# The gated sum of a decoder layer's routed experts: the next tile's products made ahead of this tile's mean, the decode tile second, slot one-hots divided 4 and 4

## The chip, the cores and the metric

One core of one Trainium2 chip runs the whole program. The core has a matrix engine (TensorE, PE in the profile), a vector engine (VectorE, DVE), an activation engine (ScalarE, ACT), a general engine (GpSimd, POOL), a sequencer for transfers (SyncE, SP) and 16 DMA engines. Each engine runs its own queue of instructions in order; between engines there are semaphores. The metric is the device time of one execution in microseconds; the median of several runs counts.

## The reference

One step of a one-layer decoder for 512 prompt tokens and 8 decode tokens that share the weights. All is float32. Cut to what matters here:

```python
x = layernorm(DN_ALPHA * x + g1 * mix, ln1_g, ln1_b)      # mix: two gated linear recurrences, merged
h = x * (1.0 + sc2) + sh2
# router: 8 of 64 experts per token, gates w (n, 8)
routed, _ = lax.scan(expert, 0, (w_exp_gate, w_exp_up, w_exp_down, gates.T))
shared = (silu(t @ w_sh_gate) * (t @ w_sh_up)) @ w_sh_down
x = layernorm(DN_ALPHA * x + g2 * (routed + shared), ln2_g, ln2_b)
```

So at the end each token takes the sum of its eight experts' outputs, each times its gate, adds the shared expert's, multiplies by `g2`, adds its residual, and is normalized over the 1024 channels.

## The kernel before, in words

The program is written for each engine by hand: a block of code per engine, whose order is the order of that engine's queue. Tokens are kept as five tiles: tiles 0 to 3 of 128 prompt tokens each, tile 4 the 8 decode tokens. The residual `X` lies channel-major (128 partitions by 8 groups of channels by 520 tokens).

**Slots of the routed loop.** The router's choices are turned into a table that says which token's row each slot of the expert loop takes. For each of the five tiles DVE computes the slot numbers (L1983 to L1993); then for each of the 8 choices k a one-hot matrix over slots is made. `PK = 5` says that POOL makes those of k = 0 to 4 (L1446) and DVE those of k = 5 to 7 (L2000). DVE also makes one wide comparison per tile (L2002, `Boh`). PE multiplies the pairs (L1078): per tile it waits for all of DVE's and then for POOL's one after another. DVE copies the table out of PSUM (L2006) and finishes it; POOL's first gathers of token rows and the first steps of the loop need it. `Aoh` and `Boh` have two buffers, so from the third tile on DVE and POOL wait for PE's products of the tile two before.

**The routed loop** runs expert by expert on all engines and stores each token's eight rows to DRAM (`yrows`). The change does not touch it.

**The final stage** starts with PE's products of the shared expert (L1174), which ACT copies to `sums[t]` (L1385). SP loads the decode tokens' rows (L807) and then `picks[t]`, 4 MB per tile, into three buffers (L812); the fourth waits until DVE has taken its half of tile 0 and PE its own. The sum over the eight choices is divided, `NPE = 4`:

- PE's half (L1195), here "gated products": 32 products of `picks` with a diagonal matrix that POOL made of the gates (L1485), into PSUM banks 0/1 or 2/3 by turns. A float32 product shows as two instructions, so the profile has 64. ACT multiplies by `g2` ("scaling", L1391, 8 operations) and POOL adds to `X` ("POOL's addition", L1491).
- DVE's half (L2074, 4 operations over 1024 channels) goes into `sums[t]`. PE transposes it (L1203, 8 operations, banks 4 and 5), and DVE adds it to `X`, times `g2` ("residual", L2082).
- The decode tile: PE multiplies the 64 rows with gates and adds the shared part (L1183, L1184, bank 6); DVE adds it in two small operations (L2064, L2066).
- The normalization of a tile: PE sums over the channels ("mean", `mean_pe`, L490, bank 6), DVE subtracts ("centre", L712), ACT squares (L569), PE sums again ("variance", `variance_pe`, L490, bank 7), ACT takes the root ("deviation", L573), DVE takes the reciprocal (L717) and multiplies (L720, both "normalize"), ACT applies weight and bias ("affine", L580), SP stores the tile (L819). Of the last tile, which carries the 8 decode tokens too, DVE does half of the affine (L2091).

PE's queue before: decode products; then for each tile t gated products t, variance t-1, transposes t, mean t; at the end variance 3. The other engines have their queues in the same sense: DVE's is decode additions, then half t, normalize t-1, residual t, centre t; ACT's is scaling t, deviation t-1, affine t-1, square t.

Of the kernel before, what the change touches and what calls it, by code (L numbers as in the profile page):

```python
# [26 lines left out]
P = 128  # L27
D = 1024
KC = D // P
SEQ = 512  # L30
DEC = 8
NT = SEQ + DEC
# [96 lines left out]
def decoder_step(nc, xT, small, wgk2, const, route, wq, wexp, st_in, yT, st_prompt, st_out):  # L129
    with ExitStack() as ctx:  # L130
# [31 lines left out]
        def view(buf, first, n, pattern=None, **kw):  # L162
            v = buf[:, first:first + n]
            return v.rearrange(pattern, **kw) if pattern else v
# [240 lines left out]
            eng.wait_ge(s_hd[0], 48)  # L405
            eng.wait_ge(s_hd[1], 32)

        PK = 5

        def visits(i, big, small, k):  # L410

# [82 lines left out]
        def mean_pe(pe, t):  # L494
            pe.wait_ge(s_f3, t + 2)
            sum_pe(pe, t, X[:, :, TAIL[t]], 6)

        def variance_pe(pe, t):
            pe.wait_ge(s_lna, t + 5)
            sum_pe(pe, t, lsq2[:, t % 2, :, 0:wide_of(t)], 7)  # L500
# [66 lines left out]
        def square_act(act, t):  # L567
            act.wait_ge(s_ln, 3 * t + 1)
            act.activation(lsq2[:, t % 2, :, 0:wide_of(t)], X[:, :, TAIL[t]], ACT.Square).then_inc(s_lna, 1)  # L569

        def deviation_act(act, t):
            act.wait_ge(s_lnp, 2 * t + 6)
            act.activation(lnr2[:, t % 2, 0, 0:wide_of(t)], ps[:, 7, t % 2 * 256:t % 2 * 256 + wide_of(t)], ACT.Sqrt,  # L573
                           bias=C("eps")).then_inc(s_lng, 1)

        def affine_act(act, t):
            g, b = S("ln2_g"), S("ln2_b")
            act.wait_ge(s_ln, 3 * t + 3)
            for c in range(KC if t < 3 else KC // 2):
                act.activation(X[:, c, TAIL[t]], X[:, c, TAIL[t]], ACT.Identity, scale=g[:, c:c + 1],  # L580
                               bias=b[:, c:c + 1]).then_inc(s_laf, 1)
# [127 lines left out]
        def centre_dve(dve, t):  # L709
            x = X[:, :, TAIL[t]]  # L710
            dve.wait_ge(s_lnp, 2 * t + 5)
            dve.tensor_tensor(x, x, wide(ps[:, 6, t % 2 * 256:t % 2 * 256 + wide_of(t)]), ALU.subtract).then_inc(s_ln, 1)  # L712

        def normalize_dve(dve, t):
            x, dev, inv = X[:, :, TAIL[t]], lnr2[:, t % 2, 0, 0:wide_of(t)], lnr2[:, t % 2, 1, 0:wide_of(t)]
            dve.wait_ge(s_lng, 4 + t)
            dve.reciprocal(inv, dev).then_inc(s_ln, 1)  # L717
            dve.wait_ge(s_ln, 3 * t + 2)
            dve.wait_ge(s_lna, t + 5)
            dve.tensor_tensor(x, x, wide(inv), ALU.mult).then_inc(s_ln, 1)  # L720
# [104 lines left out]
        def _(pe):  # L825
# [349 lines left out]
                                       shWD[:, f, hf * 512:(hf + 1) * 512], start=(f == 0), stop=(f == 1))  # L1175
                    mm.then_inc(t_y, 1)

            pe.wait_ge(s_f1[4], 16)
            pe.wait_ge(s_dg, 1)
            pe.wait_ge(t_yc, 2)  # L1180
            for m in range(KC):
                part, o = slice(m * P, (m + 1) * P), ps[:, 6, m * DEC:(m + 1) * DEC]
                pe.matmul(o, pdec[0:DEC * TOPK, part], dsel[0:DEC * TOPK, :], start=True, stop=False)  # L1183
                mm = pe.matmul(o, sums[4][0:DEC, part], ident[0:DEC, 0:DEC], start=False, stop=True)  # L1184
            mm.then_inc(s_f2, 1)
            for t in range(4):
                pe.wait_ge(s_f1[t], 16)
                pe.wait_ge(s_dg, t + 2)
                if t < 2:
                    pe.wait_ge(t_yc, 2 * TT)  # L1190
                else:
                    pe.wait_ge(s_ea, t - 1)
                for m in range(KC):
                    for k in range(NPE):
                        mm = pe.matmul(ps[:, 2 * (t % 2) + m // 4, m % 4 * P:(m % 4 + 1) * P], picks[t % 3][:, k, m * P:(m + 1) * P],  # L1195
                                       diag[:, t, k, :], start=(k == 0), stop=(k == NPE - 1))
                mm.then_inc(s_pa, 1)
                if t:
                    variance_pe(pe, t - 1)
                pe.wait_ge(s_cmb, (TOPK - NPE) * (t + 1))  # L1200
                pe.wait_ge(s_f3, t + 1)
                for m in range(KC):
                    mm = pe.transpose(ps[:, 4 + m // 4, m % 4 * P:(m % 4 + 1) * P], sums[t][:, m * P:(m + 1) * P], ident)  # L1203
                mm.then_inc(s_f2, 1)
                mean_pe(pe, t)
            variance_pe(pe, 3)


        @block.scalar
        def _(act):  # L1210
# [170 lines left out]
            for j, t in enumerate((4, 0, 1, 2, 3)):  # L1381
                rows = min(P, NT - t * P)
                for hf in range(2):
                    act.wait_ge(t_y, 2 * j + hf + 1)
                    act.activation(sums[t][0:rows, hf * 512:(hf + 1) * 512], ps[0:rows, 2 * (j % 2) + hf, :], ACT.Copy)\  # L1385
                       .then_inc(t_yc, 1)
            for t in range(4):
                act.wait_ge(s_pa, t + 1)
                since(act, s_xa, t - 1)
                for m in range(KC):  # L1390
                    ins = act.activation(gated[:, t % 2, m, :], ps[:, 2 * (t % 2) + m // 4, m % 4 * P:(m % 4 + 1) * P], ACT.Copy,  # L1391
                                         scale=md[:, G2 + m, 0:1])
                ins.then_inc(s_ea, 1)
                if t:
                    deviation_act(act, t - 1)
                    affine_act(act, t - 1)
                square_act(act, t)
            deviation_act(act, 3)
            affine_act(act, 3)

# [96 lines left out]
        def _(dve):  # L1497
# [560 lines left out]
                        gate(dve, "dve", s_y, visits(i, 2, 1, k) + (7 + hf))  # L2058
                        dve.tensor_copy(yb[:, k % 2, hf * 512:(hf + 1) * 512], ps[:, 3 if k % 2 else 4 + hf, :]).then_inc(s_yc, 1)  # L2059

            dve.wait_ge(s_laf, KC)
            dve.wait_ge(s_f2, 1)
            dec = view(tiny, 64, KC * DEC, "p (c b) -> p c b", c=KC)
            dve.tensor_tensor(dec, ps[:, 6, 0:KC * DEC].rearrange("p (c b) -> p c b", c=KC), md[:, G2:G2 + KC, 1:NCOND], ALU.mult).then_inc(s_fy, 1)  # L2064
            dve.wait_ge(s_fy, 1)
            dve.tensor_tensor(X[:, :, SEQ:NT], X[:, :, SEQ:NT], dec, ALU.add).then_inc(s_f3, 1)  # L2066
            for t in range(4):
                dve.wait_ge(s_f1[t], 16)
                dve.wait_ge(t_yc, 2 * t + 4)
                for k in range(NPE, TOPK):  # L2070
                    n = (TOPK - NPE) * t + k - NPE
                    if k > NPE:
                        dve.wait_ge(s_cmb, n)
                    dve.scalar_tensor_tensor(out=sums[t], in0=picks[t % 3][:, k, :], scalar=gk[:, t, k:k + 1],  # L2074
                                             in1=sums[t], op0=ALU.mult, op1=ALU.add).then_inc(s_cmb, 1)
                if t:
                    normalize_dve(dve, t - 1)
                dve.wait_ge(s_f2, t + 2)
                dve.wait_ge(s_xa, t + 1)
                for m in range(KC):  # L2080
                    x = X[:, m, t * P:(t + 1) * P]
                    ins = dve.scalar_tensor_tensor(out=x, in0=ps[:, 4 + m // 4, m % 4 * P:(m % 4 + 1) * P], scalar=md[:, G2 + m, 0:1],  # L2082
                                                   in1=x, op0=ALU.mult, op1=ALU.add)
                ins.then_inc(s_f3, 1)
                centre_dve(dve, t)
            normalize_dve(dve, 3)
            dve.wait_ge(s_ln, 12)
            g, b = S("ln2_g"), S("ln2_b")
# [65 lines left out]
```

## Time and profile before

| | us |
|---|---|
| median of 3 runs | 1845.16 (1844.14 to 1849.97) |
| profiled execution, its own time | 1849.65 |
| its span | 1847.8 |
| PE busy in the span | 1705.9 (92%) |
| DVE busy | 579.9 (31%) |
| ACT busy | 458.7 (25%) |
| POOL busy | 302.6 (16%) |
| mean granted clock of TensorE | 0.962 |

The span goes from the first to the last instruction of one profiled execution; its own time is what the run took as a whole. The last 100 us of the span hold the final stage, the stretch from 1017 to 1052 us the slots. The granted clock is a share of 2.4 GHz: 1.00 is 2.4 and 0.50 is 1.2 GHz.

### The profile page before, as it was taken

The page shows a single profiled execution, that of the slowest core. Times are in us where ns is not written, and L with a number is a line of the kernel's source. Part 1 is how long each engine was busy: PE and PEld are TensorE (multiplying, and loading weights), DVE is VectorE, ACT ScalarE, POOL GpSimd, SP SyncE. Part 2 cuts the span into 40 slices and gives each one's busy share as a digit, 9 for nine tenths or more (in the row PEclk, how much of TensorE's full clock was granted, in tenths as well). Part 3 has the DMA queues.
Part 4 walks back from the last instruction along what each step waited for, and adds up shares of the span by engine and source line. Part 5 has one row for each costly group of instructions (what it writes and reads, how often), then busy time and mean ns, then how long its engine had stood idle before and what let it go on. Part 6 is the DMA issues. An engine that isn't in the chain of part 4 may idle for free.

```text
span 1847.8 us, 26405 instructions
## 1 busy us (share of the span) xinstructions
PE 1705.9 (92%) x8996; PEld 1132.6 (61%) x8996; DVE 579.9 (31%) x1489; ACT 458.7 (25%) x1040; POOL 302.6 (16%) x493
## 2 busy tenths in 40 slices
PE   5999789999999899799999599999999999999975
PEld 2854468577858788588887445455444544444575
DVE  1213750586048734200136711111111111111144
ACT  1314651464145433200002111111111111111223
POOL 0000110022001100000000722222222222222311
PEclk8999989999999999899999699999999999999987
DMA  9113441211120099454011489999999999998441
GB/s 397 78 46 131 176 162 46 92 48 43 55 92 3 9 401 342 167 231 167 22 69 47 158 337 411 416 404 400 397 408 403 401 397 394 369 386 351 196 195 35
DMA packets 57197, 410.31 MB, mean 222 GB/s; under 512 B 12955, under 2 KB 18716, under 8 KB 29986
## 3 DMA queue, kind: packets, MB, share of 16 engines
q1 hardware_dynamic: 36210, 365.65, 49.9%
q0 software_dynamic: 19184, 42.58, 6.0%
q10 hardware_dynamic: 1728, 1.05, 0.2%
q8 instruction: 51, 0.84, 0.2%
q14 instruction: 24, 0.20, 0.0%
HBM read 391.79 MB, written 42.07 MB: 235 GB/s over the span
## 4 chain that ended last, share of the span: by engine, by line
PE 71%; DMA 11%; DVE 9%; ACT 5%; issue 2%; POOL 2%; SPq 0%; POOLq 0%; ACTq 0%; DVEq 0%
PE ps L957 12%; PE ps L1116 11%; PE ps L916 9%; DMA arena<-wexp 8%; PE ps L894 6%; PE ps L1121 5%; PE ps L1140 5%; PE ps L1147 3%; PE ps L997 3%; DMA arena<-wq 2%; PE ps L865 2%; PE ps L1195 2%; DVE arena L1606 2%; ACT arena L625 2%; PE ps L1102 2%
## 5 line engine op out<-in xcount | busy, mean ns | idle before, releaser
L1116 PE MATMUL ps<-arena 128*128 128x512 f32 x592 | 266.0, 603 | 10.5 <-DMA arena<-wexp 9.1
L1116 PEld LDWEIGHTS ps<-arena 128*128 128x128 f32 x592 | 111.2, 193 | 151.9 <-issue 151.9
L916 PE MATMUL ps<-Hb,arena 128*128 128x260 f32 x768 | 173.5, 390 | 0.0
L916 PEld LDWEIGHTS ps<-Hb,arena 128*128 128x128 f32 x768 | 148.8, 194 | 24.1 <-ACT arena L1251 0.5
L2050 DVE TENSOR_TENSOR arena<-ps,arena 128x256 f32<-128x256 f32 x73 | 26.2, 359 | 418.4 <-ACT arena L1365 418.4
L1469 POOL DMA_INDIRECT yrows<-arena x72 | 74.6, 1036 | 429.7 <-issue 429.7
L957 PE MATMUL ps<-Hb,arena 128*128 128x260 f32 x512 | 124.0, 397 | 14.6 <-DMA arena<-wq 14.1
L1121 PE MATMUL ps<-arena 128*64 128x256 f32 x1152 | 132.3, 382 | 1.5 <-issue 0.9
L1140 PE MATMUL ps<-arena 128*128 128x512 f32 x288 | 129.6, 592 | 0.0
L2059 DVE COPY arena<-ps 128x512 f32<-128x512 f32 x108 | 74.7, 692 | 152.1 <-PE ps L1140 105.8
L957 PEld LDWEIGHTS ps<-Hb,arena 128*128 128x128 f32 x512 | 100.8, 198 | 32.5 <-DMA arena<-wq 14.8
L1365 ACT ACTIVATE arena<-ps 128x256 f32<-128x256 f32 x73 | 24.2, 332 | 377.4 <-PE ps L1116 260.5
L865 PE MATMUL ps<-Hb,arena 128*128 128x260 f32 x512 | 117.5, 383 | 0.0
L894 PE MATMUL ps<-arena,Hb 128*128 128x512 f32 x256 | 112.0, 595 | 0.0
L1121 PEld LDWEIGHTS ps<-arena 128*64 128x64 f32 x1152 | 82.2, 137 | 41.6 <-issue 7.7
L865 PEld LDWEIGHTS ps<-Hb,arena 128*128 128x128 f32 x512 | 94.8, 190 | 13.1
L1606 DVE TENSOR_TENSOR arena<-arena 128x256 f32<-128x256 f32 x168 | 60.1, 428 | 102.7 <-ACT arena L627 102.7
L894 PEld LDWEIGHTS ps<-arena,Hb 128*128 128x128 f32 x256 | 48.0, 190 | 64.2 <-issue 60.8
L1140 PEld LDWEIGHTS ps<-arena 128*128 128x128 f32 x288 | 51.9, 190 | 51.6 <-issue 51.6
L1358 ACT ACTIVATE arena<-ps 128x512 f32<-128x512 f32 x111 | 62.4, 595 | 41.3 <-PE ps L1102 39.5
L1460 POOL DMA_INDIRECT Hb<-h2rows,arena x58 | 62.5, 1078 | 49.6 <-POOL arena L1458 47.9
L1742 DVE TENSOR_TENSOR arena<-arena,ps 128x260 f32<-128x260 f32 x32 | 13.6, 425 | 179.3 <-PE ps L957 179.2
(339 smaller groups left out, 2262.9 us busy)
## 6 DMA issues: line engine op xcount, KB each, us to landing
arena<-wexp SPq DMA_DIRECT2D x73, 2048.0 KB, 16.2
arena<-wq SPq DMA_DIRECT2D x44, 2048.0 KB, 8.5
arena<-wexp SPq DMA_DIRECT2D x72, 1024.0 KB, 19.4
arena<-yrows SPq DMA_DIRECT2D x4, 4096.0 KB, 18.8
arena<-st_in SPq DMA_DIRECT2D x8, 1024.0 KB, 10.1
Xb<-vs POOLq DMA_DIRECT2D x16, 512.0 KB, 9.8
st_out<-arena SPq DMA_DIRECT2D x8, 1024.0 KB, 9.4
Xb<-xT SPq DMA_DIRECT2D x2, 2080.0 KB, 17.6
```

What stands on the lines that cost most here:

```text
L865: mm = pe.matmul(ps[:, bank, 0:HALF], ring[:, q % 4, m % 4, c, :], H[:, c, lo:lo + HALF], start=(c == 0), stop=(c == KC - 1))
L894: mm = pe.matmul(ps[:, bank, :], H[:, c, b * P:(b + 1) * P], ring[:, q % 4, :, c, :], start=(c == 0), stop=(c == KC - 1))
L916: mm = pe.matmul(ps[:, bank, 0:HALF], ring[:, q % 4, a, c, :], H[:, c, halves[b][0]:halves[b][1]], start=(c == 0), stop=(c == KC - 1))
L957: mm = pe.matmul(ps[:, 5 + k % 3, 0:HALF], ring[:, (Q_P + n) % 4, u, c, :], (H, oa, H, ob)[u][:, c, lo:hi], start=(c == 0), stop=(c == KC ...
L1116: mm = pe.matmul(ps[:, 0, :], xe[:, 0, c, :], GU[k % 4][:, c, :], start=(c == 0), stop=(c == KC - 1))
L1121: mm = pe.matmul(ps[h * SS:(h + 1) * SS, 1, 0:FE], x, GUs[k % 4][:, c, h, :, :], start=(c == 0), stop=(c == KC - 1), tile_position=(0, h * ...
L1140: mm = pe.matmul(ps[:, 4 + hf, :], aT[:, 0, f, :], WD[k % 4][:, f, hf * 512:(hf + 1) * 512], start=(f == 0), stop=(f == 1))
L1358: act.activation(xe[:, k % 2, 4 * hf:4 * hf + 4, :].rearrange("p c n -> p (c n)"), ps[:, 6 + hf, :], ACT.Copy).then_inc(s_xc, 1)
L1460: pool.indirect_dma_start(out=xg[k % 4][:, 0:n], out_offset=None, in_=rows, in_offset=bass.IndirectOffsetOnAxis(ap=idg[:, k % 4:k % 4 + 1] ...
L1469: pool.indirect_dma_start(out=rows, out_offset=bass.IndirectOffsetOnAxis(ap=ida[:, k:k + 1], axis=0), in_=yb[:, k % 2, 0:n], in_offset=Non ...
L1606: dve.tensor_tensor(e, e, kq, ALU.mult)
L2059: dve.tensor_copy(yb[:, k % 2, hf * 512:(hf + 1) * 512], ps[:, 3 if k % 2 else 4 + hf, :]).then_inc(s_yc, 1)
```

## The change

PE's queue becomes: gated products 0, transposes 0, decode products; then for t = 0 to 2 gated products t+1, variance t-1 (from t = 1), mean t, transposes t+1; then variance 2, mean 3, variance 3. DVE's becomes: half 0, residual 0, decode additions; then for t = 0 to 2 normalize t-1 (from t = 1), half t+1, centre t, residual t+1; then normalize 2, centre 3, normalize 3. ACT's becomes: scaling 0; then for t = 0 to 2 scaling t+1, deviation t-1 and affine t-1 (from t = 1), square t; then deviation 2, square 3, affine 2, deviation 3, affine 3. POOL's and SP's queues in the final stage stay. `PK` becomes 4: POOL makes the one-hots of k = 0 to 3, DVE those of k = 4 to 7.

```diff
--- before.py
+++ after.py
@@ -405,7 +405,7 @@
             eng.wait_ge(s_hd[0], 48)
             eng.wait_ge(s_hd[1], 32)
 
-        PK = 5
+        PK = 4
 
         def visits(i, big, small, k):
 
@@ -1175,15 +1175,7 @@
                                        shWD[:, f, hf * 512:(hf + 1) * 512], start=(f == 0), stop=(f == 1))
                     mm.then_inc(t_y, 1)
 
-            pe.wait_ge(s_f1[4], 16)
-            pe.wait_ge(s_dg, 1)
-            pe.wait_ge(t_yc, 2)
-            for m in range(KC):
-                part, o = slice(m * P, (m + 1) * P), ps[:, 6, m * DEC:(m + 1) * DEC]
-                pe.matmul(o, pdec[0:DEC * TOPK, part], dsel[0:DEC * TOPK, :], start=True, stop=False)
-                mm = pe.matmul(o, sums[4][0:DEC, part], ident[0:DEC, 0:DEC], start=False, stop=True)
-            mm.then_inc(s_f2, 1)
-            for t in range(4):
+            def gated_turn(t):
                 pe.wait_ge(s_f1[t], 16)
                 pe.wait_ge(s_dg, t + 2)
                 if t < 2:
@@ -1195,14 +1187,31 @@
                         mm = pe.matmul(ps[:, 2 * (t % 2) + m // 4, m % 4 * P:(m % 4 + 1) * P], picks[t % 3][:, k, m * P:(m + 1) * P],
                                        diag[:, t, k, :], start=(k == 0), stop=(k == NPE - 1))
                 mm.then_inc(s_pa, 1)
+
+            def sums_turn(t):
+                pe.wait_ge(s_cmb, (TOPK - NPE) * (t + 1))
                 if t:
-                    variance_pe(pe, t - 1)
-                pe.wait_ge(s_cmb, (TOPK - NPE) * (t + 1))
-                pe.wait_ge(s_f3, t + 1)
+                    pe.wait_ge(s_f3, t + 1)
                 for m in range(KC):
                     mm = pe.transpose(ps[:, 4 + m // 4, m % 4 * P:(m % 4 + 1) * P], sums[t][:, m * P:(m + 1) * P], ident)
                 mm.then_inc(s_f2, 1)
+
+            gated_turn(0)
+            sums_turn(0)
+            pe.wait_ge(s_f1[4], 16)
+            for m in range(KC):
+                part, o = slice(m * P, (m + 1) * P), ps[:, 6, m * DEC:(m + 1) * DEC]
+                pe.matmul(o, pdec[0:DEC * TOPK, part], dsel[0:DEC * TOPK, :], start=True, stop=False)
+                mm = pe.matmul(o, sums[4][0:DEC, part], ident[0:DEC, 0:DEC], start=False, stop=True)
+            mm.then_inc(s_f2, 1)
+            for t in range(3):
+                gated_turn(t + 1)
+                if t:
+                    variance_pe(pe, t - 1)
                 mean_pe(pe, t)
+                sums_turn(t + 1)
+            variance_pe(pe, 2)
+            mean_pe(pe, 3)
             variance_pe(pe, 3)
 
 
@@ -1384,17 +1393,24 @@
                     act.wait_ge(t_y, 2 * j + hf + 1)
                     act.activation(sums[t][0:rows, hf * 512:(hf + 1) * 512], ps[0:rows, 2 * (j % 2) + hf, :], ACT.Copy)\
                        .then_inc(t_yc, 1)
-            for t in range(4):
+            def gated_scale(t):
                 act.wait_ge(s_pa, t + 1)
                 since(act, s_xa, t - 1)
                 for m in range(KC):
                     ins = act.activation(gated[:, t % 2, m, :], ps[:, 2 * (t % 2) + m // 4, m % 4 * P:(m % 4 + 1) * P], ACT.Copy,
                                          scale=md[:, G2 + m, 0:1])
                 ins.then_inc(s_ea, 1)
+
+            gated_scale(0)
+            for t in range(3):
+                gated_scale(t + 1)
                 if t:
                     deviation_act(act, t - 1)
                     affine_act(act, t - 1)
                 square_act(act, t)
+            deviation_act(act, 2)
+            square_act(act, 3)
+            affine_act(act, 2)
             deviation_act(act, 3)
             affine_act(act, 3)
 
@@ -2058,13 +2074,7 @@
                         gate(dve, "dve", s_y, visits(i, 2, 1, k) + (7 + hf))
                         dve.tensor_copy(yb[:, k % 2, hf * 512:(hf + 1) * 512], ps[:, 3 if k % 2 else 4 + hf, :]).then_inc(s_yc, 1)
 
-            dve.wait_ge(s_laf, KC)
-            dve.wait_ge(s_f2, 1)
-            dec = view(tiny, 64, KC * DEC, "p (c b) -> p c b", c=KC)
-            dve.tensor_tensor(dec, ps[:, 6, 0:KC * DEC].rearrange("p (c b) -> p c b", c=KC), md[:, G2:G2 + KC, 1:NCOND], ALU.mult).then_inc(s_fy, 1)
-            dve.wait_ge(s_fy, 1)
-            dve.tensor_tensor(X[:, :, SEQ:NT], X[:, :, SEQ:NT], dec, ALU.add).then_inc(s_f3, 1)
-            for t in range(4):
+            def picks_sum(t):
                 dve.wait_ge(s_f1[t], 16)
                 dve.wait_ge(t_yc, 2 * t + 4)
                 for k in range(NPE, TOPK):
@@ -2073,16 +2083,32 @@
                         dve.wait_ge(s_cmb, n)
                     dve.scalar_tensor_tensor(out=sums[t], in0=picks[t % 3][:, k, :], scalar=gk[:, t, k:k + 1],
                                              in1=sums[t], op0=ALU.mult, op1=ALU.add).then_inc(s_cmb, 1)
-                if t:
-                    normalize_dve(dve, t - 1)
-                dve.wait_ge(s_f2, t + 2)
+
+            def resid_sums(t):
+                dve.wait_ge(s_f2, t + 1 + (t > 0))
                 dve.wait_ge(s_xa, t + 1)
                 for m in range(KC):
                     x = X[:, m, t * P:(t + 1) * P]
                     ins = dve.scalar_tensor_tensor(out=x, in0=ps[:, 4 + m // 4, m % 4 * P:(m % 4 + 1) * P], scalar=md[:, G2 + m, 0:1],
                                                    in1=x, op0=ALU.mult, op1=ALU.add)
                 ins.then_inc(s_f3, 1)
+
+            dve.wait_ge(s_laf, KC)
+            picks_sum(0)
+            resid_sums(0)
+            dve.wait_ge(s_f2, 2)
+            dec = view(tiny, 64, KC * DEC, "p (c b) -> p c b", c=KC)
+            dve.tensor_tensor(dec, ps[:, 6, 0:KC * DEC].rearrange("p (c b) -> p c b", c=KC), md[:, G2:G2 + KC, 1:NCOND], ALU.mult).then_inc(s_fy, 1)
+            dve.wait_ge(s_fy, 1)
+            dve.tensor_tensor(X[:, :, SEQ:NT], X[:, :, SEQ:NT], dec, ALU.add).then_inc(s_f3, 1)
+            for t in range(3):
+                if t:
+                    normalize_dve(dve, t - 1)
+                picks_sum(t + 1)
                 centre_dve(dve, t)
+                resid_sums(t + 1)
+            normalize_dve(dve, 2)
+            centre_dve(dve, 3)
             normalize_dve(dve, 3)
             dve.wait_ge(s_ln, 12)
             g, b = S("ln2_g"), S("ln2_b")
```

## Rows read from the trace of the kernel before

**Rows 1.** Chain of waits from 1700 us: start, us, engine, tile, line, count

```profile
1748.03 0.32 PE ps L1183 x2
...
1753.80 9.69 PE ps L1195 x64
...
1763.52 2.19 ACT arena L1391 x8
...
1765.85 2.35 POOL Xb L1491
...
1768.29 2.17 DVE Xb L2082 x8
...
1770.51 3.78 PE ps L490 x16
...
1784.41 1.28 ACT L573
...
1804.60 0.27 ACT arena L573
...
1813.71 7.16 PE ps L1195 x64
```

**Rows 2.** PE's timeline: start, us, line, shapes, count, [idle before, releaser]

```profile
1763.32 1.04 PE L1203 MATMUL ps<-cst,Hb 128*128 128x128 f32 x8
...
1782.02 1.95 PE L490 MATMUL ps<-arena,cst 128*128 128x128 f32 x16
```

**Rows 3.** DVE's timeline, same columns

```profile
1754.32 5.24 DVE L2074 SCALAR_TENSOR_TENSOR Hb<-arena,OB,Hb 128x1024 f32<-128x1024 f32 x4
...
1774.33 1.22 DVE L712 TENSOR_TENSOR Xb<-Xb,ps 128x1024 f32<-128x1024 f32 x1 [3.87 <-PE ps L490]
...
1787.10 1.23 DVE L720 TENSOR_TENSOR Xb<-Xb,arena 128x1024 f32<-128x1024 f32 x1
...
1804.89 0.95 DVE L717 RECIPROCAL arena<-arena 128x128 f32<-128x128 f32 x1 [4.25 <-ACT arena L573]
1805.88 2.22 DVE L720 TENSOR_TENSOR Xb<-Xb,arena 128x1024 f32<-128x1024 f32 x1
```

**Rows 4.** ACT's timeline, same columns

```profile
1815.01 1.06 ACT L569 ACTIVATE arena<-Xb 128x1024 f32<-128x1024 f32 x1 [3.69 <-DVE Xb L712]
...
1842.02 1.67 ACT L580 ACTIVATE Xb<-Xb,sml 128x136 f32<-128x136 f32 x4 [2.40 <-DVE Xb L720]
```

**Rows 5.** Stretches: us, busy PE, PEld, DVE, ACT, POOL, granted clock, DMA share, GB/s

```profile
1748.00:1751.90 3.90, 3.90 (x27) 3.65 (x26) 0.00 (x0) 0.60 (x1) 0.00 (x0) 0.99 0.96 412
1751.90:1758.70 6.80, 6.80 (x31) 6.70 (x32) 4.64 (x6) 0.00 (x0) 0.00 (x0) 0.50 0.99 424
...
1769.00:1775.70 6.70, 5.20 (x24) 5.20 (x25) 2.83 (x8) 0.12 (x1) 0.00 (x0) 0.50 1.01 433
1813.40:1821.00 7.60, 7.60 (x70) 7.60 (x70) 6.27 (x5) 1.16 (x2) 0.00 (x0) 1.00 0.13 38
```

**Rows 6.** DMA issues at 1734.67 and 1735.30 (tiles 0, 1): KB, us to landing

```profile
arena<-yrows SPq DMA_DIRECT2D x1, 4096.0 KB, 14.0
...
arena<-yrows SPq DMA_DIRECT2D x1, 4096.0 KB, 23.0
```

**Rows 7.** One-hots: timelines of POOL, DVE, PE, and line L1446 (ns min/median/max)

```profile
1019.64 25.99 POOL L1446 TENSOR_SCALAR arena<-OB 128x128 f32<-128x128 f32 x25 [4.63 <-DVE OB L1993]
...
L1446 POOL TENSOR_SCALAR arena<-OB x25: 785/787/2127, 1019.6 to 1044.8; 128x128 f32<-128x128 f32 x25
...
1034.22 0.99 DVE L2000 TENSOR_SCALAR arena<-OB 128x128 f32<-128x128 f32 x3 [1.11 <-PE ps L1078]
...
1039.81 1.29 DVE L2002 TENSOR_TENSOR arena<-OB 128x1088 f32<-128x1088 f32 x1
1047.93 0.30 DVE L2006 COPY OB<-ps 128x136 f32<-128x136 f32 x1 [6.83 <-PE ps L1078]
...
1041.81 6.08 PE L1078 MATMUL ps<-arena 128*128 128x136 f32 x24 [1.12 <-POOL arena L1446]
```

## The prediction, as it was made

> **What bounds the kernel now.** The last 100 us are a chain over all four engines, and PE, the busiest engine of the kernel as a whole, waits in it. I read the chain of waits from 1748 us on first, then each engine's timeline there, the granted clock by stretches, the landings of the four loads, and last the stretch of the one-hots at 1019 to 1048 us.
>
> Chain, tile 0 [rows 1]: decode products from 1748.03 to 1753.80 (5.77 us), gated products 9.69, scaling on ACT 2.19, POOL's addition 2.35, DVE's residual 2.17, PE's mean products 3.78; only then tile 1's gated products. PE's own work between tile 0's gated products and that mean is 1.04 us of transposes [rows 2]: it stood idle from 1764.4 to 1770.5, and so for each tile, and its clock paid for it. In 1769.0 to 1775.7 the grant is 0.50, that is 1.2 GHz, behind such a pause; in 1813.4 to 1821.0 it is 1.00, 2.4 GHz, and 64 gated products take 7.16 us [rows 1, 5]. At 1.2 GHz sixteen mean products take 3.78 us, at 2.4 sixteen variance products 1.95 with their drain [rows 1, 2]; I use 1.75 in a filled queue, half of 3.5. The clock falls a first time at 1751.9 inside the decode products, which have 8 columns each, and so tile 0's gated products took 9.69 instead of 7.16 [rows 1, 5].
>
> The divided sum's other half, DVE's 5.24 us per tile, is always done before PE's transposes ask for it [rows 3]. The one-hots: POOL runs 25 of them without a gap for 25.99 us, DVE ends its last at 1041.1, and PE's last products at 1047.9 come behind POOL's [rows 7].
>
> **The change, part by part.** I follow the new order instruction by instruction, with the clock as these rows have it.
>
> Start. Tile 0's gated products need only tile 0's rows, landed at 1734.67+14.0=1748.67 [rows 6], ACT's copies of the shared product, which end right behind PE's, and POOL's diagonals, made long before. They start at 1748.75, directly behind wide products, so at 2.4 GHz: 7.16, to 1755.9. DVE starts its half at 1748.75 too and is done at 1754.0. Transposes 0.95, to 1756.9. Decode products: 0.315 us a pair at 2.4 GHz [rows 1], 16 pairs, 5.0, to 1761.9. Beside them run scaling (to 1758.1), POOL (to 1760.6) and DVE's residual (to 1762.8): the decode tile fills PE's pause instead of standing first. DVE's two decode additions (0.5) end at 1763.3.
>
> Tile 1's gated products start at 1761.9; their rows landed at 1735.30+23.0=1758.3 [rows 6], so no DMA wait. To 1769.1; mean of tile 0 (1.75) to 1770.8; transposes to 1771.8 (DVE's half: 1763.3 to 1768.6). Tile 2's gated products follow at once, to 1778.9, its rows should land 9.6 us behind tile 1's, at 1767.9 (an estimate from the two landings). Then variance 0 and mean 1, to 1782.4; DVE finished residual 1 at 1776.0, behind scaling and POOL.
>
> Here the new order stops giving. The first deviation comes after variance 0 and after scaling 2 (1781.1), with the table load of 1.28 [rows 1]: 1782.8. DVE has normalize 0 ahead of its half of the sum for tile 2: 0.96+1.23 [rows 3], to 1785.0, then 5.24, to 1790.3. PE's transposes of tile 2 wait for that, and behind them tile 3's products: a pause of 7.9 us. The clock will fall in it, as it did in the pause of 6.1. So transposes 1.9, to 1792.2, and gated products 3 partly at 1.2 GHz: 9.2, between 7.2 and 9.7 of [rows 1], to 1801.4. From tile 0's gated start to tile 3's it was 59.9 us, 20.0 a tile; now it is 43.4. Scaling 2.2, deviation 0.3 [rows 1], reciprocal, and a multiplication that takes 2.22 instead of 1.23 because POOL's addition lies on it [rows 3]: 1807.3. DVE's half for tile 3 to 1812.5; transposes, again after 7.6 us of pause, to 1814.5; residual 3 to 1816.7. Variance 2 (3.5, at 1.2 GHz) fills that, to 1818.4, and mean 3 needs 2.7, to 1821.2. Centre 1.22, square 1.06 [rows 3, 4], to 1823.5. Now ACT has affine 2 ahead of deviation 3: eight pieces at twice the 1.67 us of four [rows 4], about 3.2, to 1826.7; it covers variance 3 at either clock, which otherwise is 4.0. Deviation 0.36 and normalize 2.2: 1829.3. Before, that multiplication ended at 1842.0, and 5.8 us followed, which stay. The tail wins **12.7 us**.
>
> One-hots. POOL gives up 5 of 25, DVE takes 5 at about 0.29 (three cost 0.86 to 0.99) [rows 7]. POOL then needs per tile 4 times 0.787 plus the 1.34 by which DVE's wide comparison and product stretch one of its operations (2.127 against 0.787), some 4.7 with small change; DVE's 4.6 becomes 4.9. DVE's wait of 1.11 for PE [rows 7] goes, since PE is no longer held by POOL. So DVE's last comparison ends at 1041.1+5x0.29-1.11=1041.4, and PE needs for the last tile's 16 products two thirds of 6.08, 4.05 us: 1045.5 against 1047.9. The bounds: a loss of 0.3 (the 1.45 moved less 1.11), if what is late is DVE, and a gain of 3.5, if PE runs these at 2.4 GHz and only POOL's last operation, at about 1043.3, holds it. I take **2.4**, from PE's row. What follows it hangs on DVE's copy at 1047.93, gathers and expert loads alike, so the routed loop should start earlier by all of it; where the loop later waits for its loads, those were also asked for earlier.
>
> Of this the Trainium skill speaks in "GPSIMD Engine Reference", section Key points: GpSimd shares its SBUF interfaces with VectorE and contends with Vector instructions in a 2-port mode or with two SBUF inputs. The two-input side is what the 2127 ns row shows. If the moved one-hots contend as fully, the sum by the rule has no 2.4.
>
> Clock in front of tile 1. With transposes and decode products between tile 0's and tile 1's wide products, 6.0 us without a wide product, against 3.9 us from 1748.0 until the fall at 1751.9 before [rows 5], I expect it to fall there again. Tile 1's products then take 9.7, not 7.2: **2.5 back** (0 to 2.5).
>
> Sum: 1849.65 (profiled, span 1847.8 and 1.85 around it) - 12.7 - 2.4 + 2.5 = 1837.05; I say **1837.0**. The profiled execution is 4.5 above the median 1845.16 of the runs shown. I don't take that off: these runs spread over 5.8 us, which falls of the clock at shifting places of the tail would give (1.8 to 2.5 each), and the new order has fewer chances for luck. Against the median it is 8.2 us, 0.44%.
>
> **The rivals.**
> (a) The one-hots bring nothing. For: POOL's operations are stretched up to 2.7 times by DVE's. With 4x0.29 more stretch a tile, POOL needs 3.15+1.34+1.15=5.6, five tiles 28, as late as now. Against: the 25 took 25.99, 6.3 above 25x0.787, and one operation stretched by 1.34 in each of five tiles is all of that. Time 1839.4.
> (b) The tail only hides the decode tile: the ring of gated products, scaling, deviation, normalize, DVE's half, transposes is 7.2 to 9.7 + 2.2 + 0.3 + 2.2 to 3.2 + 5.2 + 1 to 1.9 = 18 to 22.5, hardly shorter than the 20.0 per tile of before. I have it twice; if it bound three times, another 6 go: 1843. For: DVE's order puts normalize ahead of the half. Against: in the first turns nothing there waits for a deviation.
> (c) Slower: PE's two pauses of almost 8 us, longer than the 6 of before, leave it at 1.2 GHz through what follows. Place: tile 1, tile 3, variance 1 and mean 2. Price: gated products at 14.3 each, 4.6 and 5.1 more, 3.5 for variance and mean, and with it one more pair for tile 2 (7.2): 20 us, 1857. It decides from 13.7 us of such loss (8.2 forecast + 5.5). Against: the two stretches at 0.50 in [rows 5] lasted 6.8 and 6.7 us, with PE at work again for 6.8 and 5.2 of them.
> (d) The change does not move the tail, because mean 0 still waits for residual 0 behind the decode additions: 0.5 us of DVE, no more; 1847.
>
> **How the numbers follow.** Forecast 0.58 (1833 to 1840), (a) 0.14, (b) 0.18, (c) 0.05, (d) 0.05. A difference under about 0.3%, 5.5 us, cannot be told from none here, so faster means below 1839.6: the forecast nearly whole, half of (a): 0.65. Within: the rest of (a), (b), part of (d): 0.27. Slower: (c) and a remainder: 0.08. Range for 8 in 10: 1831.5 (clock stays up before tile 1, one-hots at 3.5, half the median's lead) to 1844 (b).
>
> **What would show it.** Right: gated products 0 at about 1746 beginning at once behind the shared ones, lasting 7.2; decode products inside POOL's and DVE's time; three sets of gated products within 31 us; two PE pauses of 7 to 8 us ended by DVE's half of the sum; ACT's affine 2 ahead of the last deviation; DVE's table copy near 1045.5. Wrong: a pause ahead of tile 1's products, gated products of 14 us, or a copy still near 1048.

## The result and the profile after

The changed kernel takes 1832.09 us (median of 4 runs, 1830.96 to 1832.85), the kernel before beside it 1844.65. The ratio is 0.9924 with a 95% interval of 0.9907 to 0.9941, that is 14 us faster (11 to 17); the medians lie 12.6 apart. A second set of runs (below) gave 0.9934 (0.9919 to 0.9949). Forecast were 1837.0 and a gain of 8.2 us: the sign is right, the gain is half as large again, and the time lies at the lower end of the range, 1831.5 to 1844. Put on the median of 1845.16 that the forecast stood beside, the ratio gives 1831.1, just below it.

Two lines of the page of the changed kernel:

```profile
span 1828.9 us, 26402 instructions
...
PE 1690.9 (92%) x8996; PEld 1121.6 (61%) x8996; DVE 579.2 (32%) x1494; ACT 458.1 (25%) x1040; POOL 298.9 (16%) x488
```

Its profiled execution took 1830.96 us. Against the 1849.65 of before that is 18.7 less. Of the 18.9 by which the spans differ, 6.4 are ahead of the final stage (the last shared product ends at 1741.6, not 1748.0 [rows 1]) and 12.5 are in it (from there to the end of the span 87.3, not 99.8). Of the 6.4, 1.2 are there before the slots begin, 2.7 are the slots' (below), and 2.5 come in the routed loop, which is unchanged.

The chain of waits of the changed kernel, which answers to [rows 1] (start, us, engine, tile, line, count; L1187 are the gated products, L1196 the transposes, L490 mean and variance, L1400 scaling, L2084 DVE's half, L573 on ACT deviation, L712 centre, L720 normalize):

```profile
1742.38 7.38 PE ps L1187 x64
1749.76 0.87 PE ps L1196 x8
...
1755.66 8.93 PE ps L1187 x64
1764.60 1.79 PE ps L490 x16
1766.38 0.87 PE ps L1196 x8
1767.26 7.16 PE ps L1187 x64
...
1774.44 2.17 ACT arena L1400 x8
...
1776.63 1.28 ACT L573
...
1784.41 1.29 DVE Hb L2084
...
1785.75 1.97 PE ps L1196 x8
1787.72 8.15 PE ps L1187 x64
...
1804.12 1.30 DVE Hb L2084
...
1809.00 2.60 PE ps L490 x16
...
1811.63 0.38 ACT arena L573
...
1814.24 1.21 DVE Xb L712
...
1816.63 3.70 PE ps L490 x16
...
1820.36 0.38 ACT arena L573
...
1821.80 1.30 DVE Xb L720
```

Tile 0's gated products start behind the shared ones and take 7.38 us, not 9.69. Tiles 1 and 2 follow without one wait of PE's for another engine; tile 2's begin 24.9 us behind tile 0's. Then the chain leaves PE, through the first deviation, normalize and DVE's half, and does so again for tile 3. PE's timeline has both pauses in brackets:

```profile
1776.03 1.95 PE L490 MATMUL ps<-Xb,cst 128*128 128x128 f32 x16
1785.75 1.97 PE L1196 MATMUL ps<-cst,Hb 128*128 128x128 f32 x8 [7.77 <-DVE Hb L2084]
...
1806.78 1.97 PE L1196 MATMUL ps<-cst,Hb 128*128 128x128 f32 x8 [7.35 <-DVE Hb L2084]
```

They are 7.77 and 7.35 us; forecast were 7.9 and 7.6. The granted clock of four stretches (us; then busy time of PE, PEld, DVE, ACT, POOL; clock; DMA share; GB/s):

```profile
1742.40:1749.70 7.30, 7.30 (x65) 7.30 (x66) 3.78 (x3) 0.00 (x0) 0.00 (x0) 1.00 1.00 429
1755.60:1758.90 3.30, 3.30 (x16) 3.30 (x16) 3.23 (x9) 0.00 (x0) 0.00 (x0) 0.50 1.08 467
1759.00:1764.50 5.50, 5.50 (x51) 5.50 (x51) 3.20 (x3) 0.00 (x0) 0.00 (x0) 1.00 0.96 408
1782.90:1789.50 6.60, 3.75 (x18) 3.75 (x19) 5.59 (x11) 1.92 (x4) 0.00 (x0) 0.50 0.27 79
```

At 2.4 GHz through tile 0's products, at 1.2 behind the decode products (8.93 for tile 1, forecast 9.7), and at 1.2 again from inside the first pause on, until 1789.5. These rows answer to [rows 5].

The one-hots (POOL's timeline; then the line in ns, min/median/max; then DVE's timeline and PE's), against [rows 7]:

```profile
1018.42 23.25 POOL L1462 TENSOR_SCALAR arena<-OB 128x128 f32<-128x128 f32 x20 [4.61 <-DVE OB L2009]
...
L1462 POOL TENSOR_SCALAR arena<-OB x20: 784/830/2495, 1018.4 to 1040.9; 128x128 f32<-128x128 f32 x20
...
1037.09 1.26 DVE L2016 TENSOR_SCALAR arena<-OB 128x128 f32<-128x128 f32 x4
1038.18 1.28 DVE L2018 TENSOR_TENSOR arena<-OB 128x1088 f32<-128x1088 f32 x1
1044.01 0.30 DVE L2022 COPY OB<-ps 128x136 f32<-128x136 f32 x1 [4.54 <-PE ps L1078]
...
1041.73 2.24 PE L1078 MATMUL ps<-arena 8*128 8x136 f32 x10 [0.28 <-POOL arena L1462]
```

The first slot number is there at 1018.04 (1019.25 before, both by DVE's timeline). From there to the table copy L2022 it is 1044.01-1018.04=26.0 us, before 1047.93-1019.25=28.7: 2.7 less, with 2.4 forecast.

### The profile page after: what moved, and what is told of

It reads as the page before. It is cut to its first block, busy times and chain, and to the rows that moved or that the text cites. A ratio compares the mean times of both kernels' runs of the same rounds, so it can differ in the third digit from the quotient of the medians.

```text
span 1828.9 us, 26402 instructions
## 1 busy us (share of the span) xinstructions
PE 1690.9 (92%) x8996; PEld 1121.6 (61%) x8996; DVE 579.2 (32%) x1494; ACT 458.1 (25%) x1040; POOL 298.9 (16%) x488
## 4 chain that ended last, share of the span: by engine, by line
PE 69%; DMA 12%; DVE 9%; ACT 5%; issue 2%; POOL 2%; SPq 0%; POOLq 0%; ACTq 0%; DVEq 0%
PE ps L957 12%; PE ps L1116 11%; PE ps L916 9%; DMA arena<-wexp 9%; PE ps L894 6%; PE ps L1121 5%; PE ps L1140 5%; PE ps L1147 3%; PE ps L997 3%; PE ps L865 2%; DVE arena L1622 2%; ACT arena L625 2%; PE ps L1187 2%; ACT arena L627 2%; PE ps L1102 2%
## 6 DMA issues: line engine op xcount, KB each, us to landing
Xb<-xT SPq DMA_DIRECT2D x2, 2080.0 KB, 17.6
```

## The experiments

**The two parts alone.** One is a single line:

```diff
-        PK = 5
+        PK = 4
```

> The kernel before with PK = 4 alone. Theory A (the one-hots are worth the 2.4 us forecast and the loop behind them keeps it): the table copy some 2.7 us earlier against the first slot number of tile 0, and a median 2 to 4 us below the kernel before, about 1841.5. Theory B (the one-hots bring nothing, the loop waits for its loads all the same): within 1 us of the kernel before.

Measured: 0.9985 of before (0.9975 to 0.9995), 2.8 us less (0.9 to 4.6); medians 1842.46 and 1845.51. POOL's and DVE's timelines in it (L1993 the first slot number, L2006 the table copy):

```profile
1019.78 23.17 POOL L1446 TENSOR_SCALAR arena<-OB 128x128 f32<-128x128 f32 x20 [4.62 <-DVE OB L1993]
...
1019.40 0.17 DVE L1993 SCALAR_TENSOR_TENSOR OB<-OB 128x8 f32<-128x8 f32 x1
...
1045.10 0.30 DVE L2006 COPY OB<-ps 128x136 f32<-128x136 f32 x1 [4.36 <-PE ps L1078]
```

25.7 us between the two, against 28.7. Theory A holds: the loop keeps what the slots give, and rival (a) is out, by its interval only just.

> The changed kernel with PK = 5, so only the order of the final stage is new. Theory A (the sum of the prediction holds, 12.7 less 0 to 2.5 for the clock in front of tile 1): 9 to 12 us below the median of the kernel before, about 1834.5; from PE's last shared product to the end of the span about 87.5 us. Theory B (the reordered tail is worth only the hidden decode tile): 6 us below, about 1839.

Measured: 0.9952 (0.9940 to 0.9964), 8.9 us less (6.6 to 11.1), median 1836.80. From the last shared product to the end 90.9 us in its trace. That lies between the two: A had 9 to 12 us and 87.5 for the stage, B had 6 us, and the interval leaves B out only just. The parts, 2.8 and 8.9, add up to 11.7.

**The changed kernel again.**

> The changed kernel once more on this chip, for its place beside the others. Theory A (sum of the prediction taken from the usual time of the kernel before instead of its first profiled execution: 1845.5 - 12.7 = 1832.8, 1 to 2 more with the clock): 1831 to 1835. Theory B (its first four executions were lucky as the first of before was unlucky): 1835 to 1838.

Measured: 1833.93 (1830.63 to 1835.06), 0.9934, or 12.2 us less (9.4 to 15). Its final stage took 89.3 us, with tile 1's products at 9.98. Theory A, though its sum leaves the one-hots' 2.4 out; with all terms of the prediction, 12.6, it gives 1832.9.

**Where the kernel before stands.** The sum had been made on one profiled execution. The kernel before was traced three times more, unchanged.

> The kernel before once more, unchanged, for a second trace of it. Theory A (the profiled execution of 1849.65 on which the sum was made lay above what the kernel usually takes, and the spread of 1842.6 to 1850.0 comes from where the clock falls): a median of 1843 to 1846, and a trace whose stretch from PE's last shared product to the end, 99.8 us in the first trace, differs by 2 us or more if its own time does, with gated or mean products at other clocks. Theory B (1849.65 was usual, the others lucky): median 1847 or more. Theory C: the spread comes from the stretch ahead of the final stage, whose length then differs, and the 99.8 stays.

> The kernel before, one more trace. Theory A (its spread is the clock of TensorE in the final stage): if this execution's own time is 1844 or less, the stretch from the last shared product to the end is under 98 us against 99.5 to 100 in the three traces so far (1844.7 with one-hots 4 and 4, 1848.2, 1849.7). Theory C (the spread comes from the stretches ahead of it): the stretch is 99.5 to 100 again and the last shared product comes earlier.

> The kernel before, a further trace, same expectations as for the third: an execution at 1844 or less has a final stretch under 98 us by theory A and one of 99.5 to 100 by theory C.

Measured: medians of 1845.80 (11 executions of it as a kernel of its own) and 1845.51 (the 23 beside it), 1842.36 to 1849.08 in all. 1849.65 was high, above all 34 of these (of the 19 beside the later runs one took 1850.07), as theory A of the first says. But the profiled executions gave 1848.16, 1848.09 and 1848.08, all of them near the top as well, and the final stage in them is 99.5, 100.4 and 100.1 us. PE's timeline of the second trace, decode products and mean 0:

```profile
1746.58 0.39 PE L1183 MATMUL ps<-tiny,arena 64*128 64x8 f32 x2
...
1769.09 3.78 PE L490 MATMUL ps<-Xb,cst 128*128 128x128 f32 x16 [6.15 <-DVE Xb L2082]
```

The mean at 1.2 GHz again. No profiled execution of it came out low, so A and C could not be told apart by these. Over the 34 executions just named, the mean granted clock goes with the time: 13 with 0.962 or 0.963 have spans of 1844.0 to 1847.0, ten with 0.966 to 0.970 have 1840.3 to 1844.1. That fits a spread made of TensorE's time at 1.2 GHz, but it doesn't show that this is the cause, and it does not say where in the program. Two kernels with a little more PE work ahead of the final stage should say it. The first makes two of the shared products twice; the second, whose edit is not printed, makes one product more:

```diff
-                    for f in range(2):
+                    for f in ((0, 1, 0, 1) if j == 0 and hf == 0 else (0, 1)):
```

> The kernel before with two 512-column products of the shared expert made twice (1.7 us more of PE work just ahead of the final stage), nothing else. All four traces of before had the clock fall at the same distance from the last shared product (3.5 to 3.8 us) and 99.5 to 100 us of final stage; this shifts the work against the falls. Theory A (the spread of the kernel before is where the falls hit the final stage): the profiled stretch from the last shared product to the end is 3 us or more shorter than 99.5, so that the profiled execution is no slower than those of before, about 1845, though it does 1.7 us more; the median over many executions rises by 1.7. Theory C (the spread comes from ahead): the stretch stays 99.5 to 100 and the profiled execution is at 1849.8.

> The same with one product more, 0.86 us. Theory A: a stretch 3 us or more under 99.5 here as well, by other falls of the clock than with two more. Theory C: 99.5 to 100.

Measured, with two more: the profiled stage is 97.9 us, in an execution of 1845.30. PE's timeline, shared products (44 instead of 40), decode, gated products of tile 0:

```profile
1726.29 19.24 PE L1174 MATMUL ps<-OA 128*8 128x512 f32 x44 [1.15 <-DVE arena L2059]
1745.46 0.39 PE L1183 MATMUL ps<-tiny,arena 64*128 64x8 f32 x2
...
1750.49 9.04 PE L1195 MATMUL ps<-OB,arena 128*128 128x128 f32 x64
```

Median 1848.09 against 1848.07 beside it, ratio 1.0001 (0.9993 to 1.0010): 1.7 us more work, and the difference is between 1.3 us less and 1.8 more. With one more product: 100.4 us, 1848.67. So shifting the work against the falls moved the stage by 2 us in one case and not in the other. The 3 us that theory A named were not reached.

The traces say more than that when each is cut at the first slot number, at the table copy and at the end of the last shared product (us; the routed loop is counted with the shared products behind it):

| trace | own time | to the first slot number | slots | routed loop | final stage |
|---|---|---|---|---|---|
| before, first | 1849.65 | 1019.3 | 28.7 | 700.1 | 99.8 |
| before, second | 1848.16 | 1019.4 | 28.7 | 698.5 | 99.5 |
| before, third | 1848.09 | 1019.3 | 28.6 | 697.6 | 100.4 |
| before, fourth | 1848.08 | 1019.2 | 29.1 | 697.6 | 100.1 |
| two more products | 1845.30 | 1016.6 | 28.6 | 700.3 | 97.9 |
| one more product | 1848.67 | 1020.2 | 28.5 | 697.4 | 100.4 |
| changed, first | 1830.96 | 1018.0 | 26.0 | 697.6 | 87.3 |
| changed, second | 1834.09 | 1018.4 | 26.1 | 698.1 | 89.3 |

In the four traces of the kernel before the final stage differs by 1 us and the routed loop by 2.5. The 1 us follows the place where the clock falls in the decode products: not always at 3.5 to 3.8 us behind the last shared product, as expected, but by the chains of waits at 3.5, 3.8, 4.1 and 4.7, and in that order the stage takes 99.5, 99.8, 100.1 and 100.4. The 2.5 lie ahead of it; the 700.1 of the first is part of why 1849.65 was high. The low execution with two more products owes 2.6 us or more to the stretch ahead of the slots, which no edit here touches, and 1.6 to 2.5 to its final stage. So both theories have a share, and C, that the spread comes from ahead, at least as large a one as A. These runs were on another chip than those before, whose median for the kernel before is 2.3 to 2.6 higher (1848.07 against 1845.51 and 1845.81): one more reason to compare only what ran together.

**The decode tile's place.** The decode products were put first again in the changed kernel, and in the kernel before they were put into the pause ahead of mean 0. In the first, DVE's queue keeps the changed order; in the second, DVE's two decode additions move behind residual 0. Cut, the first edit is:

```diff
+            pe.wait_ge(s_f1[4], 16)
+            (decode products)
+            mm.then_inc(s_f2, 1)
             gated_turn(0)
             sums_turn(0)
-            pe.wait_ge(s_f1[4], 16)
-            (decode products)
-            mm.then_inc(s_f2, 1)
```

> The changed kernel with the decode products back at the front of PE's queue, everything else new. Theory A (in the new order PE goes from tile 0's transposes to tile 1's products without a pause, so the 5.0 us of decode products hide behind nothing and cost the same wherever they stand): within 2 us of the changed kernel, 1831 to 1835. Theory B (the prediction's words, that the decode tile fills PE's pause instead of standing first): 4 to 5 us above the changed kernel, about 1837.

Measured: 1838.35 against 1833.93 for the changed kernel on the same chip (ratios 0.9959, 0.9947 to 0.9972, and 0.9934, 0.9919 to 0.9949), 4.4 us slower. The intervals touch, but ten of its eleven executions lie above all six of the changed kernel. Theory A was mine after the result, and it fell. PE's timeline, DVE's, POOL's and PE's again, and last the fourth operation of DVE's half from the chain of waits:

```profile
1747.34 10.32 PE L1187 MATMUL ps<-OB,arena 128*128 128x128 f32 x64
...
1758.36 7.31 PE L1187 MATMUL ps<-OB,arena 128*128 128x128 f32 x64
...
1762.47 2.16 DVE L2094 SCALAR_TENSOR_TENSOR Xb<-ps,mod,Xb 128x128 f32<-128x128 f32 x8 [14.32 <-POOL Xb L1509]
...
1764.93 7.20 DVE L2086 SCALAR_TENSOR_TENSOR Hb<-arena,OB,Hb 128x1024 f32<-128x1024 f32 x4
...
1767.96 3.09 POOL L1509 TENSOR_TENSOR Xb<-Xb,arena 128x1024 f32<-128x1024 f32 x1 [5.59 <-ACT arena L1402]
...
1772.19 1.97 PE L1196 MATMUL ps<-cst,Hb 128*128 128x128 f32 x8 [4.73 <-DVE Hb L2086]
...
1768.89 3.26 DVE Hb L2086
```

Without the decode products between tile 0's and tile 1's, PE is at tile 1's transposes at 1767.5, but residual 0 begins only at 1762.47, DVE's half for tile 1 begins only behind it, and PE waits 4.73 us for it ahead of tile 1's transposes: a pause that the changed kernel does not have. The decode tile fills it. The clock is not the cause: tile 0's products take 10.32 instead of 7.38, but tile 1's take 7.31 instead of 9.98, 17.6 us in all against 17.4. And that half takes 7.20 us instead of 5.24, and POOL's addition, which lies across it, 3.09 instead of 2.35. All of DVE's loss is in the fourth operation, 3.26 instead of 1.30, the one that was to start while the addition ran. That the two contend the Trainium skill says in "GPSIMD Engine Reference", section Key points (GpSimd shares its SBUF interfaces with VectorE and contends with instructions that have two SBUF inputs). The trace agrees, and the rows have the price: 2.0 us for DVE and 0.7 for POOL.

> The kernel before with the decode products alone moved, into PE's pause between tile 0's transposes and its mean. Theory A (that pause of 6.1 us hides all of them): the 5.8 us of before go, less 0.5 for DVE's two decode additions ahead of mean 0, perhaps 2 more by a clock that no longer falls in front of tile 0's products: median 1839 to 1841. Theory B (something else starts late, the landing of tile 0's or 1's rows): 1843 or more.

Measured: 0.9969 (0.9955 to 0.9982), 5.7 us less (3.3 to 8.3), median 1840.27. PE's timeline:

```profile
1745.10 7.38 PE L1187 MATMUL ps<-OB,arena 128*128 128x128 f32 x64 [0.78 <-ACT Hb L1387]
...
1760.40 3.78 PE L490 MATMUL ps<-Xb,cst 128*128 128x128 f32 x16 [0.57 <-DVE Xb L2087]
1763.97 8.42 PE L1187 MATMUL ps<-OB,arena 128*128 128x128 f32 x64
...
1780.66 3.78 PE L490 MATMUL ps<-Xb,cst 128*128 128x128 f32 x16 [5.61 <-DVE Xb L2079]
```

The wait ahead of mean 0 is 0.57 us, not 6.15, while that ahead of mean 1 is still 5.61 by the same timeline. Theory A: this part alone is worth 5.7, nearly half of the 12.2 of the whole. The one-hots have 2.8 of the rest, so the products made ahead bring only some 3 to 5 us: 8.9 less 5.7 is 3.2 by the kernel without the one-hots, and 7.6 less 2.8 is 4.8 by the one with the decode products first (0.9959 of before). Each of these numbers is uncertain by two us or more.

**The pauses that were left.** The change made the queue of DVE wait for a deviation ahead of the half that PE needs:

```diff
+                picks_sum(t + 1)
                 if t:
                     normalize_dve(dve, t - 1)
-                picks_sum(t + 1)
                 centre_dve(dve, t)
```

> The changed kernel with DVE's half of the sum for tile t+1 queued ahead of normalize t-1, not behind it. Theory A (the two pauses of PE of 7 to 8 us are this queue order, as the forecast's ring says): both pauses gone, tiles 2 and 3 each save 6 to 7 us, less a new wait for residual 3 and its mean behind normalize 1; about 13 us below the changed kernel, 1819. Theory B (the ring is bound by scaling, deviation and POOL's addition, which the order does not touch): less than 4 us.

Measured: 1821.37 (1817.55 to 1823.17), 0.9867 of before (0.9853 to 0.9881), 24.5 us less; from the last shared product to the end 76.4 us. PE's timeline (L1187 gated products, L1196 transposes, L490 variance 2):

```profile
1771.54 7.31 PE L1187 MATMUL ps<-OB,arena 128*128 128x128 f32 x64
...
1782.26 1.04 PE L1196 MATMUL ps<-cst,Hb 128*128 128x128 f32 x8
1783.13 7.31 PE L1187 MATMUL ps<-OB,arena 128*128 128x128 f32 x64
...
1793.85 1.04 PE L1196 MATMUL ps<-cst,Hb 128*128 128x128 f32 x8
1800.86 3.75 PE L490 MATMUL ps<-arena,cst 128*128 128x128 f32 x16 [5.97 <-ACT arena L569]
```

No bracket at either set of transposes, and tile 3's products at 2.4 GHz, 7.31 against 8.15. Of the pauses that are left, the one of 5.97 us ahead of variance 2 is new; the 3.19 ahead of variance 3 was there in the changed kernel too. Theory A, to the microsecond or two. For that pause, ACT's square was put ahead of the affine as well:

```diff
                     deviation_act(act, t - 1)
-                    affine_act(act, t - 1)
                 square_act(act, t)
+                if t:
+                    affine_act(act, t - 1)
```

> The kernel with DVE's half ahead of normalize, and ACT's square t also ahead of affine t-1 in turns 1 and 2. Theory A (PE's remaining pause of 5.97 us ahead of variance 2 is square 2 waiting behind the 3.2 us of affine 1): the pause shrinks to about 3 us and the time falls by 2 to 3 us, 1818.5. Theory B (affine 1, now later, holds up normalize or the store of tile 1): no gain or a loss.

Measured: 1819.33 (1815.52 to 1820.00), 0.9859 (0.9840 to 0.9877); final stage 74.4 us. PE's timeline, the last two variances:

```profile
1793.50 3.48 PE L490 MATMUL ps<-arena,cst 128*128 128x128 f32 x16 [4.02 <-ACT arena L569]
...
1802.03 2.77 PE L490 MATMUL ps<-arena,cst 128*128 128x136 f32 x16 [3.19 <-ACT arena L569]
```

The pause is 4.02, so 2 us less, as the stage is; expected was a pause of about 3. The two intervals against before overlap, and the time alone does not settle these 2 us. It is the fastest version measured: 26 us under the kernel before, and 14.6 under the changed one beside it.

## Why the prediction was off

**The step that failed is the one from the sum to the time.** "The profiled execution is 4.5 above the median 1845.16 of the runs shown. I don't take that off": that was wrong. The base lay above all 34 executions of the second set, whose middle is 1845.5; taken from 1845.16, the same sum of 12.6 gives 1832.6, and 1832.09 and 1833.93 were measured. The reason given, that the new order "has fewer chances for luck", would have needed the changed kernel's middle to lie 12.6 under 1849.65, and it lies 12.6 under the median beside it. The reason put the spread into the tail, and the four traces of the kernel before differ there by 1 us only, in the routed loop by 2.5. The changed kernel's own profiled execution, 1830.96, was the lowest of its four, so that the two profiled ones lie 18.7 apart: some of that is luck on both sides. The bottom of the range, 1831.5, allowed for half of that lead only, and so the result came out at its edge.

**The tail.** 12.7 less 2.5, 10.2 us, against 12.5 in the first trace, 10.5 in the second (99.8 and 89.3), and 8.9 between medians with the old one-hots. The start, the order of the steps up to tile 3, both pauses and what ends them came as written. Mis-sized by a little: tile 3's products took 8.15 instead of 9.2 (8.86 in the second trace), tile 1's 8.93 and 9.98 around the 9.7, variance 2 took 2.60 instead of 3.5, and mean 3 ran at 2.4 GHz.

Two waits of the last steps came otherwise. Centre 3 was put behind mean 3; in the chain it starts at 1814.24 behind variance 2, deviation 2 and normalize 2, while mean 3 was done at 1813.45 by PE's timeline. And affine 2 was said to cover variance 3 at either clock; the prediction's own numbers, 3.2 and 4.0, don't say that, and in the chain variance 3 (3.70) ends last and releases the last deviation at 1820.36. Two of the signs were off too: the three sets of gated products took 32.0 us, not 31, since that sign leaves out the 2.5 for the clock, and the table copy came at 1044.01, not 1045.5, of which 1.2 are there before the slots begin.

**"The decode tile fills PE's pause instead of standing first".** Right, and shown twice: 5.7 us in the old order, 4.4 in the new. The pause that it fills in the new order is another than the sentence says, that ahead of tile 1's transposes, where residual 0 and DVE's half would be late.

**The one-hots.** 2.4 forecast, 2.7 in the traces, 2.8 (0.9 to 4.6) by time. The mechanism was as told but for its last step: DVE's wait of 1.11 is gone, POOL's 20 operations take 23.25, 1.5 us more per tile than 4 times 0.787, where 1.34 was forecast; the longest is now 2.495. So the moved one-hots stretch POOL's by 0.2 per tile, not by 1.15 as rival (a) had it. But the 2.4 was taken from 4.05 us of PE's products behind DVE's last comparison, and in the trace PE's last ten products take 2.24 and wait for POOL's last one-hot. That is the case which the prediction gave a gain of 3.5, so the agreement of 2.4 and 2.7 is partly luck.

**The rivals.** (b) named the ring of DVE's queue, scaling, deviation and normalize, which binds twice, as the sum had it; the kernel with DVE's half put first shows its worth, 12.4 us (0.9934 to 0.9867 of before). Its other half, that the tail only hides the decode tile, is wrong by the 3 to 5 us above. (c) had the clock at 1.2 GHz through tile 3: in the rows above it is there from 1782.9 to 1789.5, and back for the rest of tile 3's products, 8.15 us and not 14. (d) is out: PE has no wait ahead of mean 0 at 1764.60.

What stays open: how the 7 us by which the executions of one kernel part divide over the stages, since only some were traced, what makes the stretches ahead of the final stage differ, and why profiled executions of the kernel before all lay in its upper part.

## What to carry to other kernels

A sum made on a profiled execution is a difference; it belongs on the middle of many executions, above all when the profiled one lies at their edge. When the next tile's work is put ahead on one engine, read the other engines' queues for what it needs: here the matrix engine ran ahead and then stood behind the vector engine's queue, where one swap of two calls was worth as much as the whole change. A small independent piece is worth about its own length (here 5.0 us of products, worth 4.4 and 5.7) if it is put where the engine would otherwise stand.

## What the runs showed of the hardware that was not expected

A two-input operation of VectorE and an addition on GpSimd at the same time stretch each other: four of DVE's of 1.3 us took 7.20 instead of 5.24 in all, the addition 3.09 instead of 2.35. Before, in [rows 3], only DVE had paid, 2.22 instead of 1.23. There the addition was under way when DVE's operation began (1804.67 and 1805.88); here it began at 1767.96 in the middle of DVE's third.

The same kernel, unchanged, spread over 6.7 us in 34 executions, and its middle differed by 2.3 to 2.6 us between sets of runs on two chips.
